# A hybrid decoder trunk on one core: the dilated attention in two parts (neighbouring tiles, positions modulo 4) joined per pair of heads

## The reference, cut to what matters

```python
DILATED_BRANCHES = ((128, 1), (512, 4), (2048, 16))

def dilated_attention(q, k, v):
    outs = [dilated_branch(q, k, v, w, d) for (w, d) in DILATED_BRANCHES]
    ms = jnp.stack([m for _, m, _ in outs])
    ls = jnp.stack([l for _, _, l in outs])
    os_ = jnp.stack([o for o, _, _ in outs])
    wts = ls * jnp.exp(ms - jnp.max(ms, axis=0, keepdims=True))
    return jnp.einsum('gbhs,gbhsd->bhsd', wts, os_) / jnp.sum(wts, axis=0)[..., None]
```

## Time and profile before

| | |
|---|---|
| median of 3 runs | 2117.36 us (2117.34 to 2118.32) |
| the profiled execution | 2116.54 us, of it 2114.7 us span |
| PE busy | 2085.5 us, 99% |
| DVE, ACT, POOL busy | 1464.5 us (69%), 882.3 us (42%), 877.2 us (41%) |
| granted clock of PE | 0.998 of full speed |

### The profile page before, as it was taken

The page is one execution under the profiler, slowest core; times in us unless marked ns, Lnnn a source line. Parts: engine busy times, 40 slices in busy tenths (PEclk is TensorE's granted clock), DMA queues, the critical chain, the costliest instruction groups (busy, mean ns, idle before and its releaser), DMA issues.

```text
span 2114.7 us, 26180 instructions
## 1 busy us (share of the span) xinstructions
PE 2085.5 (99%) x10190; PEld 1706.5 (81%) x10190; DVE 1464.5 (69%) x1631; ACT 882.3 (42%) x1156; POOL 877.2 (41%) x456
## 2 busy tenths in 40 slices
PE   8999999999999999999999999999999999999997
PEld 6888777778888888888888888888788888888886
DVE  7668845554986677777889604537966676776988
ACT  4231434453554444444445421215544444454444
POOL 4322121123587767770001233434877677730000
PEclk9999999999999999999999999999999999999999
DMA  4101000021422222117984111213222221239872
GB/s 171 40 31 41 31 31 11 24 94 47 156 90 71 89 90 89 61 70 266 389 297 159 54 40 41 60 40 120 89 81 90 90 81 69 90 130 383 305 276 80
DMA packets 95164, 236.14 MB, mean 112 GB/s; under 512 B 10113, under 2 KB 12482, under 8 KB 95042
## 3 DMA queue, kind: packets, MB, share of 16 engines
q1 hardware_dynamic: 93170, 229.73, 30.6%
q10 hardware_dynamic: 1872, 4.74, 0.6%
...
## 4 chain that ended last, share of the span: by engine, by line
PE 89%; DVE 7%; issue 2%; ACT 1%; POOL 0%; DMA 0%; DVEq 0%; SPq 0%; ACTq 0%; POOLq 0%
PE ps L1231 12%; PE ps L1233 12%; PE ps L1232 12%; PE ps L1265 7%; PE ps L1268 7%; PE ps L1267 7%; PE ps L826 5%; PE ps L829 5%; PE ps L832 5%; PE ps L1031 2%; PE ps L1033 2%; PE ps L1032 2%; PE ps L1136 2%; PE ps L1101 1%; PE ps L1336 1%
## 5 line engine op out<-in xcount | busy, mean ns | idle before, releaser
L596 POOL TENSOR_TENSOR w_hi<-w_raw,ones 128x1024 fp32r<-128x1024 f32 x54 | 109.7, 2031 | 721.0 <-PE ps L832 228.1
L1231 PE MATMUL ps<-t_hi,w_hi 128*128 128x512 f32 x672 | 263.9, 393 | 1.7 <-ACT snap L2377 1.3
L1233 PE MATMUL ps<-t_hi,w_lo 128*128 128x512 f32 x672 | 261.7, 389 | 0.0
L1232 PE MATMUL ps<-t_lo,w_hi 128*128 128x512 f32 x672 | 261.5, 389 | 0.0
L1265 PE MATMUL ps<-d_hi 128*128 128x512 f32 (+1 forms) x640 | 244.7, 382 | 1.0 <-DVE d_lo L1944 1.0
L1267 PE MATMUL ps<-d_lo,d_hi 128*128 128x512 f32 (+1 forms) x640 | 243.9, 381 | 0.0
L1268 PE MATMUL ps<-d_hi,d_lo 128*128 128x512 f32 (+1 forms) x640 | 243.9, 381 | 0.0
L653 POOL TENSOR_TENSOR w_lo<-w_sum,w_hi 128x1024 fp32r<-128x1024 f32 x84 | 232.4, 2777 | 24.1 <-ACT w_hi L2380 24.1
L653 POOL TENSOR_TENSOR w_lo<-w_raw,w_hi 128x1024 fp32r<-128x1024 f32 x84 | 157.6, 1876 | 172.4 <-ACT w_hi L2380 158.7
L1231 PE MATMUL ps<-act_hi,w_hi 128*128 128x512 f32 x504 | 196.2, 389 | 0.3 <-POOL w_lo L653 0.3
L1232 PE MATMUL ps<-act_lo,w_hi 128*128 128x512 f32 x504 | 196.1, 389 | 0.0
...
## 6 DMA issues: line engine op xcount, KB each, us to landing
...
```

The lines of the kernel that those rows point to most:

```text
L596: pool.tensor_tensor(w_hi[:, slot, :], w_raw[:, parity, :], ones[:, 0:1].to_broadcast([P, 1024]), ALU.mult).then_inc(s_whi, 1)
L1231: pe.matmul(out, wh, bh, start=(fresh and j == 0), stop=False, skip_group_check=True)
L1232: pe.matmul(out, wh, bl, start=False, stop=False, skip_group_check=True)
L1233: ins = pe.matmul(out, wl, bh, start=False, stop=(j == 3), skip_group_check=True)
```

## The change

The softmax is cut in two parts. The **near** part (window 128) takes, for each query tile, its own and the tile before. The **far** part (windows 512 and 2048) needs only keys whose distance is a multiple of 4, so it treats the positions of one class modulo 4 together: 256 positions per class, in two blocks of 128. Each pair has 8 steps: 4 near ones of two query tiles each (512 columns; the first 384), and 4 far ones, one for each class (384 columns). The step count `g` runs to 32, `s` is the step within the pair. That is 15 near and 12 far key blocks per pair.

- K and the values are stored so that 32 positions of one class lie together (`mixed`); the queries keep their order, and a far step reads them with a stride of 4 elements (`of_class`) as the stationary operand. ACT writes a second arrangement of the values (`v_by_class`), and PE transposes them once more (`v_transposes` of `i` = 2, 3).
- DVE copies every step's output from PSUM, without a factor (`take_out`). Extremes and sums are kept (`a_stat`, `a_class`). At the end of a pair DVE puts the far ones in place by quadrant, PE moves them to the near order with 4 products of 32 columns (`move_statistics`), DVE and ACT make two factors per row from them in some 8 small operations (`statistics_differ`, `statistics_exp`, `statistics_join`), ACT spreads them in 4 chunks (`spread`), PE transposes each chunk (`factor_transposes`, 16 transposes), and DVE multiplies and adds (`combine_out`: 6 operations of 512 columns). For pairs 0 to 2 this is spread over the next pair's steps; for the last pair it stands between the last 18 pieces.
- The next pair's pieces come as K, Q, then V, 6 for each step (4 for the later steps of pair 2). The values on PE have one buffer for near and one for far, where there were two. The tables for the output projection are new.

The diff, cut to the parts that the text below speaks of:

```diff
+        def query_tiles(g):
+            hp, s = divmod(g, SA)
+            if s < NEAR:
+                return [(2 * s + u, range(max(2 * s + u - 1, 0), 2 * s + u + 1)) for u in range(2)]
+            return [(u, range(u + 1)) for u in range(2)]
...
-        WO_HIGHS = ((), (0,), (1, 2), (3,), (4,), (5,), (6,), ())
-        WO_LOWS = ((), (), (0, 1), (2,), (3,), (4,), (5,), (6,))
-        WO_PIECES = ((0,), (0,), (0,), (4,), (2, 0), (2, 0), (2, 0), (2, 2))
...
+        PIECES = ((6,) * 8, (6,) * 8, (6, 6, 6, 6, 4, 4, 4, 4), (4, 4, 0, 0, 0, 0, 0, 0))
+        WO_PIECES = (0, 0, 0, 2, 2, 2, 2, 2)
+        WO_HIGHS = ((), (), (0,), (1,), (2,), (3,), (4,), (5, 6))
+        WO_LOWS = ((), (), (0,), (1,), (2,), (3,), (4,), (5, 6))
...
                         for h in range(2):
                             rows = slice(64 * h, 64 * h + 64)
-                            ins = pe.matmul(slot2(1 + h)[:, c:c + size], q[rows, qt * P:(qt + 1) * P], k[rows, c:c + size],
-                                            start=(k is a_kh[hp % 2] and q is a_qh[hp % 2]), stop=(q is a_ql[hp % 2]))
-                            if q is a_ql[hp % 2] and c + size == keys:
+                            if s < NEAR:
+                                qs = q[rows, tile * P:(tile + 1) * P]
+                                ks = k[rows, blocks[0] * P:(blocks[-1] + 1) * P]
+                            else:
+                                qs = of_class(q[:])[rows, s - NEAR, tile * P:(tile + 1) * P]
+                                ks = by_class(k[:])[rows, s - NEAR, 0:4 * len(blocks), :]
+                            ins = pe.matmul(ps[:, 2 + h, lo:hi], qs, ks, start=(q is qh and k is kh), stop=(q is ql))
+                            if q is ql and u == 1:
                                 ins.then_inc(A.s, 1)
...
+            def move_statistics(hp):
+                pe.wait_ge(A.st, 8 * hp + 1)
+                pe.wait_ge(*((A.cm, factor_done(hp - 1, 3)) if hp else (A.vn, 5)))
+                for r in range(4):
+                    ins = pe.matmul(ps[:, 6, 0:32], lmul[:, L_LANE + 3 - r:L_LANE + 3 - r + P],
+                                    a_quad[:, r].rearrange("p t x -> p (t x)"), start=(r == 0), stop=(r == 3))
+                ins.then_inc(A.pm, 1)
...
+            def values(g):
+                hp, s = divmod(g, SA)
+                pe.wait_ge(A.ptf, 2 * g + 2)
+                pe.wait_ge(A.vn, 5 * hp + (1 if s < 2 else 2 if s < NEAR else 5))
+                if g:
+                    pe.wait_ge(A.of, g)
+                for u, (tile, blocks) in enumerate(query_tiles(g)):
+                    lo = score_cols(g, u)[0]
+                    for i, b in enumerate(blocks):
+                        for h in range(2):
+                            rows = slice(64 * h, 64 * h + 64)
+                            v = a_vn[:, b, rows] if s < NEAR else a_vc[:, 2 * (s - NEAR) + b, rows]
+                            ins = pe.matmul(ps[rows, 7, u * P:(u + 1) * P], v,
+                                            a_pt[:, 2 * (g % 2) + h, lo + i * P:lo + (i + 1) * P],
+                                            start=(i == 0), stop=(i == len(blocks) - 1))
                 ins.then_inc(A.pv, 1)
...
-            steps = [(n, gi) for n in range(PAIRS) for gi in range(groups(n))]
-            for step, (n, gi) in enumerate(steps):
-                if gi == 0 and n + 1 < PAIRS:
-                    scores(n + 1)
-                fill(n, gi)
-                transposes(n, gi, 0)
-                transposes(n, gi, 1)
-                if step:
-                    values(*steps[step - 1])
...
+            for g in range(STEPS_A):
+                hp, s = divmod(g, SA)
+                if g + 1 < STEPS_A:
+                    scores(g + 1)
+                fill(g)
+                transposes(g, 0)
+                transposes(g, 1)
+                for target, i in v_moves_of(g):
+                    v_transposes(target, i)
+                if hp and 1 <= s < 5:
+                    factor_transposes(hp - 1, s - 1)
+                if s == SA - 1:
+                    move_statistics(hp)
+                if g:
+                    values(g - 1)
+            for j in range(10, 14):
+                wo_piece(0, j)
+            values(STEPS_A - 1)
+            for j in range(0, 4):
                 wo_piece(1, j)
-            for m in range(2):
-                for j in range(14, 16):
+            for c in range(4):
+                factor_transposes(NHP - 1, c)
+                for j in range(4 + 2 * c, 6 + 2 * c):
+                    wo_piece(1, j)
+            for j in range(12, 14):
+                wo_piece(1, j)
+            for j in range(14, 16):
+                for m in range(2):
                     wo_piece(m, j)
...
+            def tops(g):
+                far = g % SA >= NEAR
+                for h in range(2):
+                    for u in range(2):
+                        lo, hi = score_cols(g, u)
+                        mask = (L_FAR if far else L_NEAR) + 2 * P
+                        if u == 0:
+                            dve.wait_ge(A.s, 2 * g + h + 1)
+                            if g >= 2:
+                                dve.wait_ge(A.pt, 2 * (g - 2) + h + 1)
+                        dve.tensor_tensor_reduce(scores_sb[:, g % 2, h, lo:hi], ps[:, 2 + h, lo:hi], lmul[:, mask - (hi - lo):mask],
+                                                 -A_SCALE, 1e30, ALU.add, ALU.min, score_stat(g, h, u, 0)).then_inc(A.max, 1)
...
+            def statistics_by_quadrant(hp):
+                dve.wait_ge(A.e, 4 * SA * (hp + 1))
+                dve.wait_ge(A.max, 4 * SA * (hp + 1))
+                if hp:
+                    dve.wait_ge(A.pm, hp)
+                dve.tensor_tensor(a_quad[:], a_class[:, hp % 2, :, None, :].to_broadcast([P, 4, 4, 8]),
+                                  lmul[:, None, L_QUAD:L_QUAD + 4, None].to_broadcast([P, 4, 4, 8]), ALU.mult
+                                  ).then_inc(A.st, 1)
...
+                dve.wait_ge(A.rt, 4 * hp + c + 1)
+                dve.wait_ge(A.of, SA * (hp + 1))
+                if which:
+                    dve.tensor_tensor(a_far[:, cols], ps[:, factor_bank(hp, c), :], a_far[:, cols], ALU.mult).then_inc(A.cm, 1)
+                    return
+                out = oT[:, hp, cols]
+                dve.tensor_tensor(out, ps[:, factor_bank(hp, c), :], near_out(hp)[:, cols], ALU.mult).then_inc(A.cm, 1)
+                dve.wait_ge(A.cm, factor_done(hp, c))
+                dve.tensor_tensor(out, out, a_far[:, cols], ALU.add).then_inc(A.cm, 1)
...
+            def take_out(g):
+                hp, s = divmod(g, SA)
+                dve.wait_ge(A.pv, g + 1)
...
+                if s < NEAR:
+                    dve.tensor_copy(near_out(hp)[:, 256 * s:256 * s + 256], ps[:, 7, 0:256]).then_inc(A.of, 1)
+                    return
+                dve.wait_ge(A.cm, 6 * hp)
+                dve.tensor_copy(of_class(a_far[:])[:, s - NEAR], ps[:, 7, 0:256]).then_inc(A.of, 1)
...
+            def attention_low(k, half=None):
+                cols = slice(0, S) if half is None else LAST[half]
+                dve.wait_ge(WO.hi, WO_ORDER.index(k) + 1 + (half or 0))
+                dve.tensor_tensor(act_lo[:, k, cols], oT[:, k, cols], act_hi[:, k, cols].bitcast(F32), ALU.subtract
+                                  ).then_inc(WO.lo, 1)
...
+            for g in range(STEPS_A):
+                hp, s = divmod(g, SA)
+                if g >= 2:
+                    take_out(g - 2)
+                if hp and s == 0:
+                    statistics_differ(hp - 1)
+                if g + 1 < STEPS_A:
+                    tops(g + 1)
+                if hp and s == 0:
+                    statistics_join(hp - 1)
+                if hp and 2 <= s < 6:
+                    combine_out(hp - 1, s - 2)
...
+                    for kk in WO_LOWS[s]:
+                        attention_low(WO_ORDER[kk])
+                if s == SA - 1:
+                    statistics_by_quadrant(hp)
+            take_out(STEPS_A - 2)
+            statistics_differ(NHP - 1)
+            statistics_join(NHP - 1)
+            take_out(STEPS_A - 1)
+            for c in range(4):
+                combine_out(NHP - 1, c)
+                if c >= 2:
+                    attention_low(NHP - 1, c - 2)
...
+            def exps(g):
+                for h in range(2):
+                    for u in range(2):
+                        lo, hi = score_cols(g, u)
+                        act.wait_ge(A.max, 4 * g + 2 * h + u + 1)
+                        at = scores_sb[:, g % 2, h, lo:hi]
+                        act.activation(at, at, ACT.Exp, scale=-1.0, bias=score_stat(g, h, u, 0),
+                                       accum_out=score_stat(g, h, u, 1)).then_inc(A.e, 1)
...
+            for g in range(STEPS_A):
+                hp, s = divmod(g, SA)
+                if hp and s == 0:
+                    statistics_exp(hp - 1)
+                if hp and 1 <= s < 5:
```

(17 more changed lines are left out.)

631 lines of the change are left out of this document (338 added, 293 removed).

## The result

The changed kernel takes **2131.27 us** (median of 4 runs, 2129.16 to 2133.48) beside 2117.35 us for the kernel before (4 runs, 2115.65 to 2118.32): a ratio of 1.0068, 95% interval 1.0056 to 1.0081. That is 13.9 us slower; the forecast was 2119.4 us, and its range ended at 2130 us.

The account below looks back on a forecast made before the run. PE bounds the kernel, busy for 2085.5 of 2114.7 us. 20.9 us saved and 23.0 us given back make the span 2.1 us longer, 2119.4 us as the median; the range with a tenth on either side is 2108 to 2130 us.

Parts of the forecast that it names:

- old waits: PE's waiting in the last pair of the kernel before, 2.9 us, counted as saved.
- new waits: PE's waits in the changed attention: 4.3 us first pair, 1.7 us third, 17.0 us last, 23.0 us in all.
- A page against the trace: Far steps' queries loaded with a stride of 4 elements: no price in the trace, none taken.
- Rival (1): Far steps: strided loads take twice as long, 144 x 0.06 = 8.6 us, 2128 us; chance 0.17.
- Rival (2): Waits weigh more: PE's clock may fall after the end's wait, or POOL's locks cost more; 2123 us, chance 0.20.
- last pair: Waits from the ring, the end's 4.8 us and POOL's splits: 17.0 us, from 9 to 22.
- The ring: Last pair from step 2: high and low part in the same step bind the engines, 5.8 us per step.
- first pair: Scores wait 2.7 us for DVE, then 1.6 us two steps on: 4.3 us, from 2 to 7.
- third pair: From step 4 DVE outlasts PE while POOL splits weights: 1.7 us of waits, from 0 to 4.
- The tail: Joining of the last pair: last low half 15.7 us after the last step, PE has 17.6 us; costed at nothing.
- (3): The ring is loose: last pair gives back 9 us, first 3 us; faster, 2110 us, chance 0.21.
- (4): PE's short groups are bound by loads, so the change doesn't save the work; costs little, no chance of its own.

Follow-up runs that it names:

- lows_lagged: Changed kernel, in the last pair statistics copies ahead of the last low parts, each low part a step behind its high part, two pieces later; 2121.27 us, ratio 1.0022.
- q_contiguous: Changed kernel with the far steps' stationary queries read contiguously, so scores of other queries are computed; 2122.6 us, ratio 1.0031.
- q_all_strided: Changed kernel with the near steps' stationary queries also read with a step of 4 elements; 2141.02 us, ratio 1.0117.
- pe_kept_busy: Changed kernel with 18 unused products of 512 columns added ahead of move_statistics in the last pair, where PE waited; 2128.03 us, ratio 1.0057.
- after_again: The changed kernel run once more with nothing edited; 2131.89 us, ratio 1.0071.
- lows_behind: lows_lagged with attention_low placed behind combine_out on DVE and no longer ahead of it; 2119.35 us, ratio 1.0008.
- loads_too: lows_behind with 8, 6, 6, 6, 6, 6, 5, 5 pieces in the first pair's steps and contiguous far queries; 2110.26 us, ratio 0.9969.

## Why the prediction was wrong

The forecast's sum was +2.1 us on the span; it was +15.6 us in the steps, and 1.4 us outside. Here is each term, for four pairs, in us, for the profiled execution, which is 2.2 us above the median. The measured column is the difference of the sums of distances between starts, kernel before against `lows_lagged`, whose products ran at the full clock but for the sixteen named (the changed kernel has the same ones); waits are those of the changed kernel, and the clock is the 8.9 us above. The terms are rounded, the sum is of the unrounded ones.

| term | forecast | measured |
|---|---|---|
| scores | -2.8 | +7.4 (-3.9 in `q_contiguous`) |
| transposes | -9.6 | -8.8 |
| value products | -10.0 | -10.6 |
| fillings | -1.6 | -1.8 |
| transposes of reciprocals | -6.4 | -6.6 |
| transposes of factors | +6.8 | +7.9 |
| transposes of values | +3.6 | +5.0 |
| products of statistics | +2.0 | +3.9 |
| old waits | -2.9 | -3.0 |
| new waits | +23.0 | +13.2 |
| clock | 0 | +8.9 |
| sum | +2.1 | +15.6 |

**The step that failed first: the strided loads, priced at nothing.** The part "A page against the trace" said that the trace gave no price and took none. Rival (1) had the mechanism and the point from which it decides, a load longer than the product before it; both `q_contiguous` and `q_all_strided` show it. Its size was right as well: 0.06 us a load, and a far step of twelve loads rose by 0.73 us; the rival's 8.6 us stand beside some 8 us of time, of 11.4 us of work on PE in all pairs. What failed is that the sum had nothing of it: without these loads (`q_contiguous`, ratio 1.0031) the kernel is inside the forecast's range. The test that the prediction named, loads' starts 0.1 us apart, was met at 0.12 us. The Trainium skill ("SBUF — State Buffer", section "Door 1: The DMA port swizzle") has a penalty for each crossing to a new line of 16 bytes and also calls a step of 4 fp32 free: the runs side with the first sentence for this step of 4, the only one that was run. A term between nothing and 8.6 us should have gone into the sum at its middle, not at its lower end.

**Second: the clock, kept out of the sum.** Rival (2) let it fall behind the one long wait at the end and priced that at some 4 us. It did fall there (2.7 us in `pe_kept_busy`), but also behind waits of 1.35 to 1.7 us at 435.6, 449.7 and 457.8 us, and in the first pair at 241.6 us. In the earlier trace rows 2.9 us of short waits had left it at 1.00, and I took that as the rule. The prediction's words "the rows neither show nor exclude it" were right; its price was half of the 8.9 us of PE's work. Of these, 5.0 us are traced to the kernel's time: 2.7 us at the end (`pe_kept_busy`), 1.6 us behind 435.6 us and 0.7 us in the first pair (both `after_again`). What the slow stretch behind 457.8 us costs wasn't measured. The Trainium skill ("TensorE: Matmul & The Clock Gate", Part 1) tells of the fall back to 1.2 GHz when PE idles, and the granted clock of 0.50 behind these waits agrees, though it didn't fall behind each: the pieces behind the wait of 1.30 us at 464.76 us were fast.

**Third: small new work, under-sized by 4.4 us.** Factors, values and statistics have 12.4 us in the forecast and cost 16.8. Their groups are short, and the entry to each new kind of work, which I had counted for the groups that went, I left out for those that came: the statistics' four products take 1.0 us (357.70 to 358.70), twice the 0.5 us that I took and at the upper end of 0 to 1. Some 0.5 us of the values are two short stops for `a_vt` (293.5 and 356.3 us) that the list of waits leaves out. The groups that went were sized well.

**The waits: the mechanism right, the size 10 us too high.** Fewer and shorter waits hid a part of the miss: that the time came out near the sum of rivals (1) and (2), 2119.4 + 8.6 + 3.6 = 2131.6 us, is luck, since the clock took more than (2) says and the waits less. In the *last pair* they stood where the forecast had them: for `act_lo` at the first piece, 1.35, 0, 1.58, 1.73 and 1.30 us in steps 3 to 7 (forecast 2.3, 1.2, 1.3, 2.0, 2.8), and 4.17 us ahead of `move_statistics` (4.8). With two waits of 0.3 us, for `a_far` and `a_vt`, it is 10.8 us, not 17.0. The ring was no fixed 5.8 us: `act_hi` started 7.0, 5.55, 8.34, 8.36 and 5.1 us apart, because strided scores and slow products made PE's part longer than forecast, and because two low parts met POOL's splits (2.88 and 2.59 us in place of 1.23), as forecast. A slower PE waits less, so these terms aren't independent, and a sum that adds them as if they were overstates. In the *first pair* it was one wait of 1.63 us, not 2.7 and 1.6, and a step earlier than forecast: the scores of step 2 wait for the rope of the queries' second half (`a_ql`), which I had put down as done. In the *third pair* there was none, forecast 1.7. The 0.8 us for `a_quad` at the end of the first two pairs (294.91 and 357.70 us) weren't in the forecast.

**The tail: right.** Its chain never stalls PE. No wait stands in the list behind 476 us. The forecast put the low half's end at 15.7 of 17.6 us and saw 2 us of cover; it was closer: the last low half ends at 492.29 us (491.60 + 0.69), and the piece that needs it starts at 492.51.

**What rivals (3) and (4) got.** (4), that the work isn't saved, is nearly what pair 1 shows: 62.8 us for its steps (279.99 to 342.81) beside 63.0 before (279.03 to 342.03), where the forecast said 58. But the cause isn't short groups as such: in `q_contiguous` that pair takes 59.9 us. (3) is refuted as a forecast, since the ring is there, and `lows_behind` shows what it is worth when it's loosened: 13 us with the clock behind it.

What stays open: why the clock falls behind a given wait in one run and not in the next, and at which other steps a strided load gets dearer. And the three causes don't add up exactly by runs (1.0070 to 0.9969 is 21 us; loads 11.4, clock 8.9 and waits 13.2 would be 33 us), since a part of the loads and of the slow products only takes the place of waiting, and 8.8 us of waits and twelve slow products are left in `loads_too`.
